# Eight units of two experts ahead of the first unit of one, and one expert's down weights issued later

## The reference

```python
def swiglu(x, wg, wu, wd):
    return (jax.nn.silu(x @ wg) * (x @ wu)) @ wd

def moe(h, p):
    ...
    _, eidx = lax.top_k(masked, TOP_K)          # 8 of 64 experts for each token
    ...
    def expert_block(args):
        xb, e = args
        return swiglu(xb, wg[e], wu[e], wd[e])  # 1024 -> 256 -> 1024
    ...
    shared = swiglu(h, p['sh_w_gate'], p['sh_w_up'], p['sh_w_down'])
    return (shared.astype(f32) + routed).astype(h.dtype)
```

## Time and profile before

| | |
|---|---|
| runs (three) | 1730.41, 1730.71, 1733.8 us; median 1730.71 us |
| profiled execution | 1731.37 us; span of its instructions 1729.5 us |
| TensorE matmul busy | 1583.1 us (92%) |
| VectorE busy | 840.1 us (49%) |
| DMA: weights and other plain loads | 503.90 MB |
| DMA: gathered rows | 25.22 MB |
| memory read over the span | 533.76 MB |

### The profile page before, as it was taken

How to read it: one execution, slowest core, us unless ns; L and a number is a source line. 1 busy time by engine, 2 the same in 40 slices (tenths; PEclk the granted TensorE clock), 3 DMA queues, 4 the chain that set the end, 5 groups by cost and what they waited for, 6 DMA issues and landing times.

```text
span 1729.5 us, 22727 instructions
## 1 busy us (share of the span) xinstructions
PE 1583.1 (92%) x7900; PEld 791.3 (46%) x7900; DVE 840.1 (49%) x2813; ACT 346.4 (20%) x776; POOL 425.5 (25%) x421
## 2 busy tenths in 40 slices
PE   6999899899998998888979997998999899889886
PEld 2865355544443434434347553554444344344333
DVE  3777553644443443444165856455444434343332
ACT  2501443111111111111152014431111111111111
POOL 0300010143332332333013000004333323332320
PEclk9999999999999999999989999999999999999998
DMA  9322825779999999999632239028999999999993
GB/s 398 142 104 98 345 105 195 292 290 413 413 413 413 413 412 412 413 413 414 285 128 98 104 104 395 1 82 333 369 412 412 416 413 412 412 414 413 413 415 141
DMA packets 80851, 530.59 MB, mean 307 GB/s; under 512 B 13968, under 2 KB 17308, under 8 KB 25184
## 3 DMA queue, kind: packets, MB, share of 16 engines
q1 hardware_dynamic: 67680, 503.90, 71.9%
q0 software_dynamic: 13056, 25.22, 4.0%
HBM read 533.76 MB, written 5.77 MB: 312 GB/s over the span
## 4 chain that ended last, share of the span: by engine, by line
PE 58%; DMA 31%; DVE 6%; issue 2%; SPq 2%; ACT 1%; POOL 0%; DVEq 0%; ACTq 0%
PE PSB L946 21%; DMA WB<-in_exp_w_up 21%; DMA RING<-in_exp_w_up 8%; PE PSB L938 7%; PE PSB L959 6%; PE PSB L874 4%; PE PSB L993 2%; PE PSB L994 2%; PE PSB L689 2%; PE PSB L910 1%; PE PSB L920 1%; PE PSB L911 1%; PE PSB L933 1%; SPq L517 1%; PE PSB L732 1%
## 5 line engine op out<-in xcount | busy, mean ns | idle before, releaser
L946 PE MATMUL PSB<-RING,EX 128*32 128x512 f32 (+2 forms) x1344 | 409.1, 608 | 44.9 <-DMA WB<-in_exp_w_up 31.1
L946 PE MATMUL PSB<-WB,EX 128*32 128x512 f32 (+2 forms) x1408 | 417.8, 600 | 30.1 <-DMA RING<-in_exp_w_up 23.3
L564 POOL DMA_INDIRECT XG<-h_rows,IDX x272 | 279.0, 1026 | 181.2 <-issue 94.4
L959 PE MATMUL PSB<-RING,AT 128*32 128x512 f32 (+2 forms) x720 | 227.0, 598 | 4.8 <-ACT GROW L1298 3.7
L572 POOL TENSOR_SCALAR SCAT<-CST,LSTT 128x384 fp32r<-128x384 f32 x68 | 84.9, 1248 | 561.3 <-PE PSB L994 561.1
L946 PEld LDWEIGHTS PSB<-WB,EX 128*32 128x32 f32 (+2 forms) x1408 | 128.2, 127 | 191.1 <-issue 191.1
L946 PEld LDWEIGHTS PSB<-RING,EX 128*32 128x32 f32 (+2 forms) x1344 | 123.2, 128 | 199.0 <-issue 199.0
L959 PE MATMUL PSB<-WB,AT 128*32 128x512 f32 (+2 forms) x704 | 210.8, 596 | 0.0
L1852 DVE TENSOR_TENSOR YL<-PSB,YH 128x512 fp32r<-128x512 f32 x136 | 94.0, 691 | 186.0 <-ACT YH L1378 186.0
L1776 DVE COPY LCOL<-PSB 128x6 f32<-128x6 f32 x68 | 11.2, 164 | 345.8 <-PE PSB L977 312.8
L993 PE MATMUL PSB<-YH,SCAT 128*128 128x512 f32 x408 | 171.8, 421 | 2.8 <-DVE YL L1852 2.8
(11 more groups left out here) (287 smaller groups left out, 1832.5 us busy)
## 6 DMA issues: line engine op xcount, KB each, us to landing
RING<-in_exp_w_gate SPq DMA_DIRECT2D x64, 1024.0 KB
RING<-in_exp_w_up SPq DMA_DIRECT2D x64, 1024.0 KB
RING<-in_exp_w_down SPq DMA_DIRECT2D x64, 1024.0 KB, 20.6
WB<-in_exp_w_gate SPq DMA_DIRECT2D x64, 1024.0 KB, 16.6
WB<-in_exp_w_up SPq DMA_DIRECT2D x64, 1024.0 KB, 20.6
WB<-in_exp_w_down SPq DMA_DIRECT2D x64, 1024.0 KB, 20.7
RING<-in_wmod SPq DMA_DIRECT2D x16, 2048.0 KB, 11.2
KSYS<-in_wmod SPq DMA_DIRECT2D x8, 2048.0 KB, 10.5
```

The lines of the kernel that those rows point to most:

```text
L564: pool.indirect_dma_start(XG[:, s % 2, g * 256:(g + 1) * 256], None, h_quarters, bass.IndirectOffsetOnAxis(ap=IDX[:, s, g:g + 1], axis=0), ...
L946: mm = nc.tensor.matmul(PS[6][s0:s0 + w, :].rearrange("p (w f) -> p w f", w=2), e(k, s0, w), rawgu[n % NBUF][:, k], start=(k == 0), stop=( ...
L959: mm = nc.tensor.matmul(dst[s0:s0 + w, :], AT[:, j, s0:s0 + w], rawdn[n % NBUF][:, hf, j], start=(j == 0), stop=(j == 1))
```

## The change

The order of the units in `WIDE` becomes another: eight pairs stand first, and the four singles (30 to 33) follow at places 8, 15, 22 and 29. Before, singles stood at places 0, 1, 8 and 16. Which experts share a unit doesn't change, nor what is computed. Second, when the expert n = 4 belongs to the unit being loaded, SP leaves its down weights out and issues them together with those of the next unit, behind that unit's gate and up weights. With the new order n = 4 is the second expert of unit 1, and the next unit is the third one, unit 2.

```diff
-        WIDE = (30, 31) + tuple(range(0, 6)) + (32,) + tuple(range(11, 18)) + (33,) + tuple(range(6, 11)) + tuple(range(18, 30))
+        WIDE = (tuple(range(0, 6)) + (11, 12, 30) + tuple(range(13, 18)) + (6, 31) + tuple(range(7, 11)) + (18, 19, 32)
+                + tuple(range(20, 26)) + (33,) + tuple(range(26, 30)))
...
                 sp.wait_ge(d_ord, l + 1)
+                late = []
                 for s, job in enumerate(JOBS):
                     es = [sp.value_load(ORD[0:1, p[1]:p[1] + 1], min_val=0, max_val=NE - 1) for p in job]
                     for (n, c, cap, tiles), e in zip(job, es):
...
                         sp.dma_start(raw[b][:, 2048:4096], row(I["exp_w_up"], l, e)).then_inc(gu_in[b], 16)
-                    for (n, c, cap, tiles), e in zip(job, es):
+                    for (n, c, cap, tiles), e in late + list(zip(job, es)):
                         b = n % NBUF
+                        if n == NBUF and s == OWNER[n]:
+                            late = [((n, c, cap, tiles), e)]
+                            continue
                         free(l, n, True)
                         sp.dma_start(raw[b][:, 4096:6144], row(I["exp_w_down"], l, e)).then_inc(dn_in[b], 16)
+                    if s > OWNER[NBUF]:
+                        late = []
```

## The result

The changed kernel takes 1722.38 us (median of 4 runs, 1719.96 to 1725.04) against 1731.14 us for the kernel before, measured beside it (4 runs, 1730.41 to 1733.8). The ratio is 0.9937, with a 95% interval of 0.9919 to 0.9955: some 10.9 us less, between 7.8 and 14.0; the two medians alone are 8.8 us apart, inside this interval. The prediction said 1720 us, 1714 to 1727. The profiled execution is the slowest of its four, 1725.04 us, with a span of 1723.2 us.

A forecast was written before the change was run, and what follows sets the result against it. The sixteen DMA engines were taken to bound the mixtures, losing time at the openings. Layer 0's 4.2 us and layer 1's 6.7 us, together 10.9, off 1731.4 give 1720.5, less 0.7 for the median: 1720 us, range 1714 to 1727.

The forecast's parts named there:

- The bound and the size: DMA engines set the pace; standing still at both layers' openings loses 26.2 us, of which the change wins 10.9 us.
- The two openings: Starts of both layers' mixtures, losing 12.8 and 13.4 us before; the change leaves 8.6 and 6.7 us lost.
- the length of unit 0's product: Gate and up product of each layer's first unit, taken as unchanged: 9.20 and 7.11 us.
- the moment at which the holes open: From 346 us in layer 0 and 1194 us in layer 1, only gathers move, at 73 and 103 GB/s.
- The two times from product to issue: SP issues gate and up of n = 5 and 6 0.2 us behind unit 0's product, at 354.8 and 1201.1.
- The other holes: Second and third hole of each opening close, smallest queue reserve 5 us; windows there at 400 GB/s or more.
- The singles: In the DMA-bound stretch the queue covers them, 0.1 us lost; rival of costly singles: 1741 us at 5.3 each, chance 0.09.
- The bounds of 0.1 and 5.3 us: Loss per single in the DMA-bound stretch: 0.1 us if the queue covers it, up to 5.3 if loads come late.
- The late down weights: Expert 4's, issued later: out of the queue by 370.0, TensorE may stand a microsecond in unit 1; 3.3 us gained.
- The rival in which they land 8 us late: Late down weights land near 379, TensorE stands 8 us in unit 1; 1720 to 1724 us; chance within the forecast's 0.68.
- The first wait for up weights: TensorE's first wait for up weights in layer 0 comes at unit 4, near 403 us.
- The ends: Last two units of each layer: up to 4.4 us less without slow last-but-one products, up to 2.7 more with another.

The follow-up runs named there:

- e5: Changed kernel with each layer's four singles in a row at places 15 to 18; 1736.4 us, ratio 1.0032 to the kernel before.
- e7: Changed kernel with the fourth single at the last place (places 8, 15, 22 and 33); 1732.89 us, ratio 0.9996 to the kernel before.
- e6: Changed kernel with the singles two by two, at places 15, 16, 23 and 24; 1721.18 us, ratio 0.9932 to the kernel before.
- e1: Changed kernel without the late down weights, so the new order of units alone; 1726.0 us, ratio 0.9958 to the kernel before.
- e3: The changed kernel again, unaltered, as a control and for a second profile; 1720.06 us, ratio 0.9927 to the kernel before.
- e8: Changed kernel without late weights, the shared expert's last down product moved ahead of unit 0; 1715.89 us, ratio 0.9905 to the kernel before.

## Why the prediction was right, point by point

**The bound and the size.** The two openings were to lose 8.6 + 6.7 = 15.3 us and lost 5.8 + 7.6 = 13.4, so 12.8 us were won there and not 10.9. By layer it is further off: 4.2 and 6.7 us were forecast, 7.0 and 5.8 were won. What shifted it between the layers is the length of unit 0's product, which I took as unchanged: in layer 0 it took 7.07 us instead of 9.20, in layer 1 9.02 instead of 7.11. The granted clock was 0.83 around the first of these long products and 0.85 around the second (the window from 1194 us above), 1.00 around the short ones, so part of both stretches ran at the lower of the clock's two levels. That is no gain of the change, and over both layers it cancels but for 0.2 us. Of the other 1.7 us, 1.3 come from the moment at which the holes open. The prediction let them open at 346 and 1194 us, edges of windows, but earlier loads still moved then, and seen from unit 0 they end later in the changed kernel; why isn't shown. In the four windows of 1 us from 345 on (349.44 here) they moved 397, 306, 154 and 16 GB/s instead of 367, 208, 45 and 0, which is 0.6 us of full rate, and in the five from 1192 on 0.7 us more than before. The two times from product to issue were right, 0.2 us each. So the mechanism was right, and that the measured ratio gives the forecast's 10.9 us is luck in part: the mixtures of the profiles are 14.8 us shorter, and the clock put a long product into one opening of each profile.

**The other holes** closed as worked out: 415 GB/s from 360 and from 1206 us, where 400 was asked. From 1203 us, the prediction's own mark, it is 396, as unit 0's product ended 1.9 us later there than forecast.

**The singles** cost nothing measurable where the change puts them: 412 and 413 GB/s over the two full stretches, and of the windows of 10 us from 394 and from 1206 on none within 80 us behind a single, the ends of the layers apart, is under 402. The bounds of 0.1 and 5.3 us each both have their place. In e5, eight singles in rows of four cost 16 to 18 us, 2 us each; in e7, one at the end of each layer costs 5 to 6 us, the size of the upper bound, though on TensorE and not on the DMA engines; one alone, or two on end, with pairs behind them, stay near the lower one. So the choice was right, and e5 and e6 fit the reason given, the depth of the queue.

**The late down weights** came just in time. In unit 1 TensorE's down product stands where it needs them (timeline of TensorE; start us, us, what, and in brackets the idle time before):

```profile
374.26 0.63 PE L966 MATMUL PSB<-WB,AT 128*32 128x512 f32 x3 [0.42 <-issue]
...
1220.21 0.63 PE L966 MATMUL PSB<-WB,AT 128*32 128x512 f32 x3 [0.43 <-issue]
```

0.4 us in each layer, where the prediction allowed a microsecond. The profile names no releaser, but the last of the sixteen completions of this load stands in the trace at 374.17 and at 1220.12, 0.09 us ahead. The rival in which they land 8 us late is out. Their share of the gain was to be 3.3 us and the order's 7.6; e1 measured 7.3 us for the order, and e1 against e3 5.4 us for the late weights, too uncertain to tell from 3.3.

By the Trainium skill ("DMA: Bandwidth & Descriptors", Rules for kernel authors), a DMA is issued early and waited on late. By it the old place would have been kept. e1 against e3 speaks for the late place, as the prediction held (5.4 us, with an uncertainty of 4.1). But e8 agrees with the rule: with the wait ahead of the transfer ended sooner, the early place is likely better than the late one, by 4 to 5.5 us in the ratios.

**The first wait for up weights** was forecast for unit 4 and came at unit 3, at 392.81. Its weights landed at 371.91 + 20.81 = 392.72; the forecast had them at 388.8, 393.2 with the 4.4 us by which this execution is later, so the load came as forecast. TensorE was sooner: unit 0's product took 2 us less than I had taken. It stood for 0.90 us, and that costs nothing, as the DMA engines were at full rate by then.

**The ends.** The slow last-but-one products of before, 9.83 and 8.79 us, didn't recur. These are the first and the last matmul of that product in layers 0 and 1 (timeline of TensorE):

```profile
836.79 0.61 PE L953 MATMUL PSB<-RING,EX 128*64 128x512 f32 x1 [1.34 <-DMA WB<-in_exp_w_up]
...
843.29 0.59 PE L953 MATMUL PSB<-WB,EX 128*64 128x512 f32 x1
...
1677.89 0.61 PE L953 MATMUL PSB<-RING,EX 128*64 128x512 f32 x1 [0.77 <-DMA WB<-in_exp_w_up]
...
1684.39 0.59 PE L953 MATMUL PSB<-WB,EX 128*64 128x512 f32 x1
```

843.29 + 0.59 - 836.79 is 7.1 us, although TensorE had waited 1.34 us ahead of it, and 1684.39 + 0.59 - 1677.89 is 7.1 us too. The openings' 12.8 us and the mixtures' 14.8 differ by 2.0 us, inside the 4.4 that the prediction gave these ends. Whether the ends did it isn't shown; in e7 such a product came back (8.78 us). The last products themselves start 3.8 and 6.5 us earlier in the span, where 4 and 11 were forecast, since the code ahead of and between the mixtures took longer in this execution. The median of the first four runs is 8.8 us lower, that of the second set 12.5. What separates these from the mixtures' 14.8 us isn't shown; the rest of the span, which the change doesn't touch, varies from 713.6 to 722.4 us between the profiles of before, of the changed kernel and of e1 to e7, and the lowest is the one profile of before.

## What to carry to other kernels

Where the DMA engines set the pace at full rate, count what they lose at the openings in time at full rate, and look for the instruction at which the issuing queue stands: a wait there delays every load behind it, and here the time grew by what was lost. When units differ in bytes per unit of compute time, start with those that free the most buffers, put the others singly or in twos into the DMA-bound stretch, and keep some heavy ones for the end: the same four units of each layer cost nothing, or some 16 us, or 11, by their places. And before a transfer is moved behind a wait, see whether the wait itself can end earlier: here that was likely worth more than the detour around it.

## What the runs showed of the hardware

The sixteen DMA engines don't end together. Where the last weights of layer 0 are through, the changed kernel's windows of 2 us read (columns as in the earlier trace rows):

```profile
844.00:846.00 2.00, 2.00 (x11) 1.65 (x10) 0.91 (x2) 0.30 (x1) 0.00 (x0) 1.00 1.02 418
846.00:848.00 2.00, 2.00 (x12) 0.97 (x12) 0.00 (x0) 0.39 (x1) 0.80 (x1) 1.00 0.75 315
848.00:850.00 2.00, 2.00 (x12) 0.66 (x10) 0.35 (x1) 0.60 (x1) 0.44 (x1) 1.00 0.46 193
850.00:852.00 2.00, 1.04 (x6) 0.23 (x4) 0.98 (x2) 0.60 (x1) 0.00 (x0) 1.00 0.37 156
852.00:854.00 2.00, 2.00 (x12) 0.86 (x10) 0.06 (x1) 0.00 (x0) 0.00 (x0) 1.00 0.22 90
854.00:856.00 2.00, 2.00 (x12) 0.72 (x9) 0.00 (x0) 0.00 (x0) 0.00 (x0) 1.00 0.06 25
```

The share falls from 1.02 to 0.06 over ten microseconds, although the last loads were issued at 835.93. The trace has sixteen completions for this last load: the first at 847.2 us, ten by 849.9, the sixteenth at 856.5, and the load has landed only with that one. The up load that starts the last unit has its last completion at 851.6, where the chain has 851.56. The kernel before shows the same fall, from 340 to 25 GB/s between 846 and 858 us. From 846 to 856 us 6.2 us of full rate are lost. The spread isn't the same in every kernel: from the first to the sixteenth completion of layer 0's last load it is 9.3 us here, 12.7 in the kernel before, and 6.1 and 6.4 in e5 and e6. Why it differs isn't shown.

And TensorE's granted clock isn't the same from execution to execution at the same place of the same code: 0.79 and 1.00 from 220 to 240 us in two executions of the changed kernel. Outside the mixtures these two differ by 6.7 us (722.1 and 715.4). A gain of 10 us is read safely from two single profiles only if the stretch that the change touches is measured by itself.
